# The last value group of a PEER layer: block by block over eight banks, with its norm's rows read earlier

## The chip, the cores and the metric

One core of one Trainium2 chip. The metric is the device time of one execution in microseconds (us); lower is better. TensorE multiplies matrices, VectorE and ScalarE work on rows and columns in SBUF (on-chip memory) and PSUM (the eight banks that TensorE writes), GpSimd gathers rows, and SyncE's queue issues most of the transfers.

## What is computed

A decoder layer for 512 tokens of width 2048: a mixer of attention and a state space model, a first layer norm, and a PEER feed-forward layer with a second layer norm. The change touches the end of the last part:

```
h   = x * (1 + sc2) + sh2
act = gelu(h @ u_tab[ids].T)          # 128 picked experts of 16384 for each token
ffn = (g * act) @ v_tab[ids]
x   = LN2(ALPHA * x + (1 + g2) * ffn)  # mean, variance, gain, shift over 2048 columns
```

## The kernel before, in words

Tokens stand in four blocks of 128 (TB = 4). For three of them (DB = 3, 384 tokens) the feed-forward runs densely over all 16384 experts, as 128 tiles of 128 experts, with gates that are zero for experts not picked. The fourth block is done by gathered rows, and its norm ends earlier.

The 128 tiles go in 32 groups of 4 (GT = 4), and `stream()` makes every engine walk the same list of groups. A group of kind "full" has 16 units: four u units, four v units, four u, four v. A unit is 512 KB (128x1024 f32) of the table, loaded by SyncE's queue (L725) into one of four slots `raw` when an earlier unit's split (`unit_split`) has freed it. It is split into two fp32r parts: `unit_high` on ScalarE copies the high part (L1125), `unit_low` on VectorE subtracts (L1780), into `split[:, j % 2]`. The high part of unit j waits until unit j-2 is used. A u unit is half the contraction of one tile of experts (matmuls L2212, bank 6 or 7, weights `h2_parts`). A v unit (L2276) is one tile of experts and one half of the 2048 output columns: 18 matmuls of 512 columns, three row blocks of six, added up in banks 0 to 5 (`bank_of`: block m in banks 2m and 2m+1). After four v units VectorE adds the banks to `out4` (`add_values`, L1710), counted by `v_read`, and TensorE's next unit waits for each block's read. In VectorE's `group()` the second half of a group is added at j = 0 to 3 of the next.

The last group ("last") has only the eight v units of the tiles before: units 0 to 3 are the left half of the columns, 4 to 7 the right half. TensorE runs unit by unit, each over the three blocks. `add_values` of the left half stands at j = 4. When SyncE has issued all loads and the full groups are used, it reads the first norm's output rows of the three blocks (`x1_back`, 3 MB, in the space of `h2_parts`, L733). VectorE's in-order list then is:

```
unit_low(5); first_half(0); unit_low(6); first_half(1); unit_low(7); first_half(2)
second_prepared(0..2)
second_half(0); second_half(1); finished(0); second_half(2); finished(1); finished(2)
```

`first_half(m)` (L1747, L1748, L1554) waits for `x1_back`, multiplies the left half of a row block by the gate row `g2b`, adds `x1_back`, and takes statistics of it. `second_prepared` (L1754, L1755) does the product and the sum for the right half. `second_half` (L1845, L1846) waits for all eight units, multiplies the right half's banks by the gate, adds, takes statistics and calls `spread` (L1422 to L1424). ScalarE takes the square root (`spread_root`, L1050). `finished` (L1561 to L1563, L1567, L1568) refines the root and applies mean, gain and shift; SyncE stores the rows. `own(...)` is an operation that VectorE waits for before the next.

## Time and profile before

| | us |
|---|---|
| median of 3 timed runs | 3253.71 (3250.67 to 3255.66) |
| the profiled execution | 3245.96 |
| its span in the trace | 3244.2 |
| granted TensorE clock, mean | 0.983 of 2.4 GHz |
| last u unit used, last unit of the full groups used, last matmul | 3147.5, 3164.95, 3204.94 |
| VectorE's last operation | 3239.92 |

The page gives busy times over the whole span. Since several stages with different limits follow each other, the end is read from three other views: the chain of waits in order of time (what released the work that ended last), the timeline (what ran when, and what ended an idle time), and busy times in stretches. All times of the trace are from the span's start.

### The profile page before, as it was taken

Reading aid. Unit: us, or ns where it says so; the run is one execution under the profiler, and the core shown is the slowest. Engines: PE = TensorE matmul, PEld = TensorE weight load, DVE = VectorE, ACT = ScalarE, POOL = GpSimd, SP = SyncE. Lnnn points to the kernel's source line nnn. Section 1 sums busy time; section 2 is a strip of 40 time slices with the busy share of each in tenths; the row PEclk is TensorE's granted clock in tenths of the full one; section 3 lists DMA queues with packets and bytes.
Section 4 is the critical chain, followed back from the end, with each engine's and each line's share of the span. In section 5 each row is a group of like instructions: output and inputs, shape, how many; then the busy total and the mean of one; then the engine's idle time right before and its main releaser. Section 6 shows DMA issues by size and latency. Waiting matters only on the chain.

```text
span 3244.2 us, 43813 instructions
## 1 busy us (share of the span) xinstructions
PE 3109.5 (96%) x16016; PEld 2659.8 (82%) x16016; DVE 2455.2 (76%) x3452; ACT 1056.3 (33%) x1632; POOL 1026.5 (32%) x734
## 2 busy tenths in 40 slices
PE   6999999999999999999999999999999999999994
PEld 4778887666469999997777899998999999999983
DVE  2397655645639999978888777888888888888757
ACT  1323545422223334332223333333333323333331
POOL 0110000000026553523222233435555554545200
PEclk9999999999999999999999999999999999999997
DMA  9786114465144555459888888888999899988853
GB/s 363 283 297 227 59 59 158 167 242 187 56 155 136 181 169 196 155 196 336 284 295 284 273 275 297 301 309 319 341 336 338 303 333 337 337 314 325 286 174 117
DMA packets 277725, 795.07 MB, mean 245 GB/s; under 512 B 118272, under 2 KB 138960, under 8 KB 230864
## 3 DMA queue, kind: packets, MB, share of 16 engines
q1 hardware_dynamic: 218816, 465.73, 42.6%
q0 software_dynamic: 50560, 317.87, 26.2%
q10 hardware_dynamic: 8208, 9.56, 0.8%
q8 instruction: 92, 1.51, 0.2%
q14 instruction: 49, 0.40, 0.0%
HBM read 750.07 MB, written 43.02 MB: 244 GB/s over the span
## 4 chain that ended last, share of the span: by engine, by line
PE 75%; DVE 18%; DMA 3%; issue 2%; ACT 1%; SPq 0%; POOL 0%; DVEq 0%; POOLq 0%; ACTq 0%
PE ps L2276 28%; PE ps L2212 26%; PE ps L1935 12%; DVE arena L1685 4%; PE ps L2187 3%; DVE arena L1682 2%; DMA arena<-in_w_ada 1%; DVE arena L1263 1%; PE ps L1959 1%; DVE arena L1710 1%; DVE split L1780 1%; PE ps L1894 1%; PE ps L1994 1%; PE ps L1871 1%; DVE win_parts L1250 1%
## 5 line engine op out<-in xcount | busy, mean ns | idle before, releaser
L2276 PE MATMUL ps<-split,w_parts 128*128 128x512 f32 x4608 | 1070.9, 392 | 20.0 <-DVE split L1780 17.2
L2276 PEld LDWEIGHTS ps<-split,w_parts 128*128 128x128 f32 x4608 | 863.8, 188 | 216.8 <-DVE split L1780 19.0
L2212 PE MATMUL ps<-h_parts,split 128*128 128x384 f32 x5376 | 947.4, 335 | 2.0 <-POOL split L788 1.4
L2212 PEld LDWEIGHTS ps<-h_parts,split 128*128 128x128 f32 x5376 | 933.7, 188 | 5.9 <-issue 1.6
L1125 ACT ACTIVATE split<-below_parts 128x1024 fp32r<-128x1024 f32 x416 | 441.7, 1062 | 1203.3 <-PE ps L2276 711.6
L1780 DVE TENSOR_TENSOR split<-below_parts,split 128x1024 fp32r<-128x1024 f32 x416 | 509.2, 1224 | 256.7 <-ACT split L1125 251.7
L800 POOL COPY arena<-arena 128x1 uint32 x256 | 209.8, 819 | 694.8 <-DVE arena L1734 389.4
L1715 DVE CUSTOM_DVE_ANT_0 arena<-arena 128x2048 f32<-128x2048 f32 x128 | 293.2, 2291 | 22.8 <-DMA arena<-in_u_tab,arena 22.8
L1734 DVE SCALAR_TENSOR_TENSOR arena<-arena 128x2048 f32<-128x2048 f32 x128 | 300.6, 2349 | 4.3 <-DVE arena L1726 2.2
L803 POOL DMA_INDIRECT arena<-in_v_tab,arena x128 | 257.4, 2011 | 104.4 <-POOL arena L800 103.1
L1250 DVE TENSOR_TENSOR win_parts<-arena,win_parts 128x512 fp32r<-128x512 f32 (+2 forms) x208 | 128.3, 629 | 210.5 <-ACT win_parts L854 201.3
L788 POOL TENSOR_TENSOR split<-below_parts,split 128x1024 fp32r<-128x1024 f32 x64 | 174.5, 2727 | 324.1 <-ACT split L1088 324.1
L803 POOL DMA_INDIRECT arena<-in_u_tab,arena x128 | 232.3, 1815 | 109.1 <-POOL arena L800 102.1
L1710 DVE TENSOR_TENSOR arena<-arena,ps 128x1024 f32<-128x1024 f32 x189 | 225.9, 1215 | 29.0 <-PE ps L2276 29.0
L1935 PE MATMUL ps<-win_parts,h_high_part 128*128 128x512 f32 (+1 forms) x640 | 198.7, 379 | 6.3 <-DVE win_parts L1250 4.2
L854 ACT ACTIVATE win_parts<-arena 128x512 fp32r<-128x512 f32 (+2 forms) x208 | 117.0, 576 | 194.1 <-PE ps L1935 187.5
L1685 DVE TENSOR_SCALAR arena<-iota,arena 128x128 f32<-128x128 f32 x384 | 169.5, 511 | 0.0
L755 POOL DMA_DIRECT2D arena<-in_w_slices x56 | 29.8, 533 | 406.0 <-DVE win_parts L1250 406.0
L1935 PEld LDWEIGHTS ps<-win_parts,h_high_part 128*128 128x128 f32 x640 | 118.4, 189 | 31.2 <-DVE win_parts L1250 7.5
L2212 PE MATMUL ps<-h_parts,w_parts 128*128 128x384 f32 x768 | 139.6, 336 | 0.9 <-PE ps L1959 0.6
L1935 PE MATMUL ps<-h_high_part,win_parts 128*128 128x512 f32 x384 | 132.9, 410 | 5.3 <-DVE h_low_part L1238 5.3
L2212 PEld LDWEIGHTS ps<-h_parts,w_parts 128*128 128x128 f32 x768 | 133.0, 188 | 1.7 <-issue 1.0
(275 smaller groups left out, 3221.2 us busy)
## 6 DMA issues: line engine op xcount, KB each, us to landing
below_parts<-in_u_units SPq DMA_DIRECT2D x256, 512.0 KB, 4.7
below_parts<-in_v_tab SPq DMA_DIRECT2D x256, 512.0 KB, 6.9
arena<-in_w_ada SPq DMA_DIRECT2D x96, 1024.0 KB, 7.2
arena<-in_w_slices POOLq DMA_DIRECT2D x56, 512.0 KB, 4.6
gates_by_expert<-arena SPq DMA_DIRECT2D x24, 1024.0 KB, 4.8
below_parts<-gates_by_expert SPq DMA_DIRECT2D x32, 768.0 KB, 9.1
arena<-in_w_out POOLq DMA_DIRECT2D x32, 512.0 KB, 5.5
acts_ahead<-arena ACTq DMA_DIRECT2D x48, 192.0 KB, 2.1
```

Source lines behind the costliest of these rows:

```text
L788: nc.gpsimd.tensor_tensor(part[:, 1, :], pre_raw[:, n % PRE_RAWS, :], part[:, 0, :].bitcast(F32), ALU.subtract).then_inc(pre_split, 1)
L800: nc.gpsimd.tensor_copy(idx[:, slot:slot + 1], ids[:, DB, bass.ds(pick, 1)]).then_inc(idx_copied, 1)
L803: nc.gpsimd.indirect_dma_start(out=ring[slot], out_offset=None, in_=table[:, :], in_offset=bass.IndirectOffsetOnAxis(ap=idx[:, slot:slot + ...
L1125: nc.scalar.activation(split[:, j % 2, 0, :], raw[:, j % RAWS, :], ACT.Copy).then_inc(high_done, 1)
L1685: ins = nc.vector.tensor_scalar(hot[:, 1, t, :], iota[:, :], pick_cols[:, 1, at_t:at_t + 1], pick_cols[:, 2, at_t:at_t + 1], ALU.is_equal, ...
L1710: nc.vector.tensor_tensor(row, row, wide(g.bank_of(-half if before else half, m), UNIT), ALU.add).then_inc(v_read, 1)
L1715: nc.vector.tensor_tensor_reduce(out=ring[slot], in0=ring[slot], in1=h2_now, scale=1.0, scalar=0.0, op0=ALU.mult, op1=ALU.add, accum_out=a ...
L1734: nc.vector.scalar_tensor_tensor(acc_v, ring[slot], w4[:, q:q + 1], acc_v, ALU.mult, ALU.add).then_inc(row_used, 1)
L1780: nc.vector.tensor_tensor(split[:, j % 2, 1, :], raw[:, j % RAWS, :], split[:, j % 2, 0, :].bitcast(F32), ALU.subtract)\
L1935: return nc.tensor.matmul(ps[:, bank_at, 0:cols], lhs, rhs, start=first and q == 0, stop=last and q == 2)
L2212: ins = nc.tensor.matmul(ps[:, 6 + b, 0:DT], lhs[:, cols], h2_parts[:, rhs, k, :], start=k == 0 and n == 0, stop=k == KT - 1 and n == 2)
L2276: ins = nc.tensor.matmul(ps[:, g.bank_of(half, m) + b, :], w_parts[:, buf, lhs, i, m * P:(m + 1) * P], rhs[:, b * 512:(b + 1) * 512], star ...
```

## The change

It concerns the last group and the norm behind it.

- SyncE issues the read of `x1_back` behind the load of the last group's unit 0, as soon as unit 11 (the last u unit) of the last full group is used.
- `prepared(m)` does product and sum of whole rows (2048 columns) before any unit of the last group is added, at j = 1, 2, 3, behind the split of that unit.
- The units 5 and 6 are split into spare space behind `x1_back`, so that their splits wait for no unit; unit 7 waits for units 0 to 3.
- TensorE does units 0 to 3 as before, in banks 6/7, 0/1, 2/3; then the right half block by block, all four units for block 0, 1 and 2, in banks 4/5, 6/7, 0/1.
- `half_whole(g, half, m)` multiplies a block's half out of PSUM by the gate and adds it to the row, with an operation that also gives the sum of the result. It takes the place of `add_values`, `second_half` and the statistics. `row_mean` makes the mean of the two sums.
- ScalarE gives the sum of squares about the mean (Square with the negative mean as bias and a sum over the row), written over `x1_back`; `row_spread` makes the variance of it.
- Two semaphores are replaced by counts of others (`gate_row_ps` by `gate_row`, `firsts_set` by `c_made`), with the same waits.

The diff, without the last of these:

```diff
@@ -287,6 +287,8 @@
+        if self.kind == "last" and half >= 0:
+            return (6 - 2 * half + 2 * m) % 8
         turned = self.c if half >= 0 else self.c - 1
@@ -531,6 +533,13 @@
         gated_part = at(PARTS + WP + UP + DB * D, UNIT)
+        spare_split = [h2_parts.rearrange("p a b c -> p (a b c)")[:, DB * D + UNIT + 2 * UNIT * i:DB * D + UNIT + 2 * UNIT * (i + 1)]
+                       .rearrange("p (a b) -> p a b", a=2) for i in range(2)]
+
+        def split_of(g, j):
+
+            return spare_split[j - 5] if g.kind == "last" and j in (5, 6) else split[:, j % 2, :, :]
+
         gate_tile = arena[0:3 * KT, LATER_ACC:LATER_ACC + P]
@@ -723,14 +732,15 @@
                     sp.dma_start(raw[:, slot, :], what.rearrange("a p n -> (a p) n")).then_inc(raw_full[slot], 16)
+                    if g.kind == "last" and j == 0:
+                        sp.wait_ge(unit_used, Group("full", GROUPS - 1, at_share=3).unit(12))
+                        sp.dma_start(x1_back, x1_out[:, 0:DB, :]).then_inc(x1_moved, 16)
                 if g.second:
...
-            sp.wait_ge(unit_used, Group("last", GROUPS).unit(0))
-            sp.dma_start(x1_back, x1_out[:, 0:DB, :]).then_inc(x1_moved, 16)
             for n, m in enumerate(TAIL):
@@ -1120,9 +1130,11 @@
                     act.wait_ge(pre_used, EARLY - 2 + j)
-                else:
+                elif g.kind == "last" and j == 7:
+                    act.wait_ge(unit_used, g.unit(4))
+                elif not (g.kind == "last" and j in (5, 6)):
                     act.wait_ge(unit_used, g.unit(j - 1))
-                nc.scalar.activation(split[:, j % 2, 0, :], raw[:, j % RAWS, :], ACT.Copy).then_inc(high_done, 1)
+                nc.scalar.activation(split_of(g, j)[:, 0, :], raw[:, j % RAWS, :], ACT.Copy).then_inc(high_done, 1)
@@ -1172,6 +1184,8 @@
             for n, m in enumerate(TAIL[1:]):
+                act.wait_ge(row_whole, n + 1)
+                nc.scalar.activation(x1_back[:, m, :], out4[:, m, :], ACT.Square, bias=mv[:, m, 1:2], accum_out=spread_of[:, m:m + 1]).then_inc(row_squared, 1)
                 spread_root(m, 2 * TB + 1 + n)
@@ -1738,21 +1752,36 @@
-            def first_half(m):
+            def prepared(m):
...
                     dve.wait_ge(x1_moved, 32)
-                    dve.wait_ge(v_read, (2 * GROUPS - 1) * DB)
-                part = out4[:, m, 0:UNIT]
-                own(nc.vector.tensor_tensor(part, part, g2b[:, 0:UNIT], ALU.mult))
-                own(nc.vector.tensor_tensor(part, part, x1_back[:, m, 0:UNIT], ALU.add))
-                half_stats(m, out4[:, m, :], 0)
-
-            def second_prepared(m):
-
-                part = out4[:, m, UNIT:]
-                own(nc.vector.tensor_tensor(part, part, g2b[:, UNIT:], ALU.mult))
-                own(nc.vector.tensor_tensor(part, part, x1_back[:, m, UNIT:], ALU.add))
+                    dve.wait_ge(v_read, (2 * GROUPS - 2) * DB)
+                row = out4[:, m, :]
+                own(nc.vector.tensor_tensor(row, row, g2b, ALU.mult))
+                own(nc.vector.tensor_tensor(row, row, x1_back[:, m, :], ALU.add))
+
+            def half_whole(g, half, m):
+
+                dve.wait_ge(unit_used, g.unit(4 + half * (m + 1)))
+                cols = slice(half * UNIT, (half + 1) * UNIT)
+                part = out4[:, m, cols]
+                nc.vector.tensor_tensor(gated_part, wide(g.bank_of(half, m), UNIT), g2b[:, cols], ALU.mult).then_inc(v_read, 1)
+                dve.wait_ge(v_read, g.val(2 * DB, (half - 1) * DB + m + 1 - DB))
+                own(nc.vector.tensor_tensor_reduce(out=part, in0=part, in1=gated_part, scale=1.0, scalar=0.0,
+                                                   op0=ALU.add, op1=ALU.add, accum_out=stats[:, m, half, 0:1]))
+
+            def row_mean(m):
+
+                left, right = stats[:, m, 0, 0:1], stats[:, m, 1, 0:1]
+                nc.vector.tensor_scalar(mv[:, m, 0:1], left, right, 1.0 / D, ALU.add, ALU.mult)
+                nc.vector.tensor_scalar(mv[:, m, 1:2], left, right, -1.0 / D, ALU.add, ALU.mult).then_inc(row_whole, 1)
+
+            def row_spread(m):
+
+                dve.wait_ge(row_squared, m + 1)
+                own(nc.vector.tensor_scalar(spread_of[:, m:m + 1], spread_of[:, m:m + 1], 1.0 / D, EPS, ALU.mult, ALU.add))
+                nc.vector.reciprocal(inv_root[:, m:m + 1], spread_of[:, m:m + 1]).then_inc(var_ready, 1)
@@ -1777,7 +1806,7 @@
                 dve.wait_ge(high_done, g.unit(j + 1))
-                nc.vector.tensor_tensor(split[:, j % 2, 1, :], raw[:, j % RAWS, :], split[:, j % 2, 0, :].bitcast(F32), ALU.subtract)\
+                nc.vector.tensor_tensor(split_of(g, j)[:, 1, :], raw[:, j % RAWS, :], split_of(g, j)[:, 0, :].bitcast(F32), ALU.subtract)\
                     .then_inc(unit_split, 1)
@@ -1812,7 +1841,7 @@
                                 add_values(g, 1, m, g.unit(0), True)
-                            if j == 4:
+                            if j == 4 and g.kind != "last":
                                 add_values(g, 0, m, g.unit(4))
@@ -1827,31 +1856,29 @@
                         gathered_block(j)
-                    if g.kind == "last" and j >= 5:
-                        first_half(j - 5)
+                    if g.kind == "last" and 1 <= j <= DB:
+                        prepared(j - 1)
+                    if g.kind == "last" and j == 7:
+                        for m in range(DB):
+                            half_whole(g, 0, m)
...
-            for m in range(DB):
-                second_prepared(m)
-
-            def second_half(m):
-
-                dve.wait_ge(unit_used, Group("last", GROUPS).unit(8))
-                part = out4[:, m, UNIT:]
-                own(nc.vector.tensor_tensor(gated_part, wide(2 * m, UNIT), g2b[:, UNIT:], ALU.mult))
-                own(nc.vector.tensor_tensor(part, part, gated_part, ALU.add))
-                own(half_stats(m, out4[:, m, :], 1))
-                spread(m)
-
-            second_half(0)
-            second_half(1)
+            last = Group("last", GROUPS)
+            half_whole(last, 1, 0)
+            row_mean(0)
+            half_whole(last, 1, 1)
+            row_mean(1)
+            row_spread(0)
             finished(0)
-            second_half(2)
+            row_spread(1)
+            half_whole(last, 1, 2)
+            row_mean(2)
             finished(1)
+            row_spread(2)
             finished(2)
@@ -2256,6 +2283,8 @@
                 for j, (table, i, half) in enumerate(g.units):
+                    if g.kind == "last" and half:
+                        continue
                     pe.wait_ge(unit_split, g.unit(j + 1))
@@ -2269,13 +2298,30 @@
                                 pe.wait_ge(pre_gelu, AHEAD * GT)
-                            if i == 0 and not (g.second and (half == 0 or m == 0)):
+                            if i == 0 and g.kind == "last":
+                                if m == 0:
+                                    pe.wait_ge(tile_gelu, g.val(GT, 2 - AHEAD * GT))
+                                else:
+                                    pe.wait_ge(v_read, g.val(2 * DB, m - 3 * DB))
+                            elif i == 0 and not (g.second and (half == 0 or m == 0)):
                                 pe.wait_ge(v_read, g.val(2 * DB, (half - 2) * DB + m - DB + (0 if g.kind == "ahead" else 1)))
...
                     ins.then_inc(unit_used, 1)
+                if g.kind == "last":
+                    for m in range(DB):
+                        pe.wait_ge(v_read, g.val(2 * DB, m - 2 * DB))
+                        for i in range(GT):
+                            j = GT + i
+                            pe.wait_ge(unit_split, g.unit(j + 1))
+                            high, low = split_of(g, j)[:, 0, :], split_of(g, j)[:, 1, :]
+                            for n, (lhs, rhs) in enumerate(((0, high), (0, low), (1, high))):
+                                for b in range(2):
+                                    ins = nc.tensor.matmul(ps[:, g.bank_of(1, m) + b, :], w_parts[:, buf, lhs, i, m * P:(m + 1) * P], rhs[:, b * 512:(b + 1) * 512],
+                                                           start=i == 0 and n == 0, stop=i == GT - 1 and n == 2)
+                        ins.then_inc(unit_used, 1)
```

## Rows read from the trace of the kernel before

**Rows 1.** The page: span, and busy time of each engine.
```profile
span 3244.2 us, 43813 instructions
...
PE 3109.5 (96%) x16016; PEld 2659.8 (82%) x16016; DVE 2455.2 (76%) x3452; ACT 1056.3 (33%) x1632; POOL 1026.5 (32%) x734
```

**Rows 2.** The chain of waits, 3050 to 3245 us: start us, us, what.
```profile
3177.62 12.23 DMA arena<-x_rows
3189.88 1.24 DVE arena L1747
```

**Rows 3.** The timeline of the last group: start us, us, engine, line, operation [idle before <-releaser].
```profile
3164.99 3.48 DVE L1710 TENSOR_TENSOR arena<-arena,ps 128x1024 f32<-128x1024 f32 x3 [1.70 <-PE ps L2276]
...
3166.36 16.61 PE L2276 MATMUL ps<-split,w_parts 128*128 128x512 f32 x72 [1.41 <-DVE arena L1710]
3168.39 1.22 DVE L1780 TENSOR_TENSOR split<-below_parts,split 128x1024 fp32r<-128x1024 f32 x1
...
3193.60 1.21 DVE L1780 TENSOR_TENSOR split<-below_parts,split 128x1024 fp32r<-128x1024 f32 x1
3193.99 1.28 ACT L1050 ACT_TABLE_LOAD   x1
3194.72 1.22 DVE L1747 TENSOR_TENSOR arena<-arena 128x1024 f32<-128x1024 f32 x1
...
3194.86 10.08 PE L2276 MATMUL ps<-split,w_parts 128*128 128x512 f32 x36 [2.04 <-DVE split L1780]
```

**Rows 4.** The timeline of the tail.
```profile
3210.82 1.23 DVE L1845 TENSOR_TENSOR arena<-ps,arena 128x1024 f32<-128x1024 f32 x1
3212.08 1.23 DVE L1846 TENSOR_TENSOR arena<-arena 128x1024 f32<-128x1024 f32 x1
...
3215.14 0.16 DVE L1424 RECIPROCAL arena<-arena 128x1 f32<-128x1 f32 x1
3215.22 1.21 DVE L1845 TENSOR_TENSOR arena<-ps,arena 128x1024 f32<-128x1024 f32 x1
...
3229.28 0.20 DVE L1561 SCALAR_TENSOR_TENSOR arena<-arena 128x1 f32<-128x1 f32 x1
...
3234.55 0.21 DVE L1561 SCALAR_TENSOR_TENSOR arena<-arena 128x1 f32<-128x1 f32 x1
...
3237.57 2.35 DVE L1568 SCALAR_TENSOR_TENSOR arena<-arena 128x2048 f32<-128x2048 f32 x1
```

**Rows 5.** Two rows of the timeline, and the value loads' row of the DMA view.
```profile
3147.48 4.28 PE L2276 MATMUL ps<-split,w_parts 128*128 128x512 f32 x18
...
3152.35 25.23 SPq L725 DMA_DIRECT2D below_parts<-in_v_tab  x7
...
below_parts<-in_v_tab SPq DMA_DIRECT2D x12, 512.0 KB, 4.1
```

**Rows 6.** Groups on VectorE by shape: operation xcount | busy us, mean ns.
```profile
L1715 DVE CUSTOM_DVE_ANT_0 arena<-arena 128x2048 f32<-128x2048 f32 x128 | 293.2, 2291 | 22.8 <-DMA arena<-in_u_tab,arena 22.8
...
L1715 DVE DVE_READ_ACCUMULATOR2_ANT arena<- 128x1 f32 x128 | 10.6, 83 | 0.0
...
L1762 DVE TENSOR_TENSOR arena<-arena 128x2048 f32<-128x2048 f32 x1 | 2.3, 2282 | 0.0
```

**Rows 7.** ScalarE: a group of 2048 columns, and the timeline of an Exp (L908) and a Square (L914).
```profile
L974 ACT ACTIVATE arena<-arena 128x2048 f32<-128x2048 f32 x1 | 1.9, 1917 | 0.0
...
535.65 0.63 ACT L908 ACTIVATE arena<-arena 128x512 f32<-128x512 f32 x1
536.18 0.62 ACT L914 ACTIVATE arena<-arena 128x512 f32<-128x512 f32 x1
536.71 0.18 ACT L914 ACTIVATION_READ_ACCUMULATOR arena<-arena 128x1 f32 x1
```

**Rows 8.** Busy time in stretches; PEclk, DMA share and GB/s last.
```profile
3148.00:3165.00 17.00, 16.34 (x71) 12.82 (x69) 9.29 (x10) 4.88 (x6) 0.00 (x0) 1.00 0.39 118
...
3196.00:3198.00 2.00, 2.00 (x6) 1.60 (x5) 1.97 (x3) 0.00 (x0) 0.00 (x0) 0.50 0.03 8
```

More of the change, by code:

```diff
@@ L567, in decoder_layer @@
             "cols_ps cols_ready hot_ready g_ps g_staged pre_high pre_split pre_used pre_gelu high_done unit_split unit_used "
-            "tile_gelu w_made w_high w_ready v_read picks_w tail_loaded gate_row_ps gate_row gate_stored ada_row firsts_set x1_ready y_ready "
+            "tile_gelu w_made w_high w_ready v_read picks_w tail_loaded row_whole gate_row gate_stored ada_row row_squared x1_ready y_ready "
             "out_done var_ready root_ready"
@@ L577, in decoder_layer @@
          pre_high, pre_split, pre_used, pre_gelu, high_done, unit_split, unit_used, tile_gelu, w_made, w_high, w_ready, v_read,
-         picks_w, tail_loaded, gate_row_ps, gate_row, gate_stored, ada_row, firsts_set, x1_ready, y_ready, out_done, var_ready,
+         picks_w, tail_loaded, row_whole, gate_row, gate_stored, ada_row, row_squared, x1_ready, y_ready, out_done, var_ready,
          root_ready) = map(sem, names.split())
@@ L646, in _ @@
                 weights(slot, w_q[slot, :, :])
-            sp.wait_ge(gate_row, 1)
+            sp.wait_ge(gate_row, 2)
             sp.dma_start(rows_out[:, :], gate_tile).then_inc(gate_stored, 16)
@@ L981, in beside @@
                 if n == TURNED + 1:
-                    act.wait_ge(gate_row_ps, 1)
+                    act.wait_ge(gate_row, 1)
                     nc.scalar.activation(gate_tile, ps[0:3 * KT, 6, 0:P], ACT.Copy).then_inc(gate_row, 1)
@@ L1189, in _ @@
             own(nc.vector.tensor_tensor(firsts[:, :], firsts[:, :], ident[:, 64:65], ALU.add))
-            nc.vector.tensor_tensor(firsts[:, :], firsts[:, :], ident[:, 96:97], ALU.add).then_inc(firsts_set, 1)
+            nc.vector.tensor_tensor(firsts[:, :], firsts[:, :], ident[:, 96:97], ALU.add).then_inc(c_made, 1)
             dve.wait_ge(small_loaded, 9 * 16)
@@ L2138, in beside @@
                     pe.wait_ge(mod_ready, CHUNKS + MODS - 2)
-                    turn(ps[0:3 * KT, 6, 0:P], mod_cols[:, 3 * KT:6 * KT]).then_inc(gate_row_ps, 1)
+                    turn(ps[0:3 * KT, 6, 0:P], mod_cols[:, 3 * KT:6 * KT]).then_inc(gate_row, 1)
             pe.wait_ge(c_made, 2)
@@ L2144, in _ @@
             pe.wait_ge(consts, 18)
-            pe.wait_ge(firsts_set, 1)
+            pe.wait_ge(c_made, 3)
             chunk_mod_sums(0)
@@ L2171, in _ @@
                 if m == 0:
-                    pe.wait_ge(gate_row, 1)
+                    pe.wait_ge(gate_row, 2)
                 if m == 1:
```

## The prediction, made before the changed kernel was run

> **What bounds the kernel now.** The page comes first: TensorE is busy 96% of the span, VectorE 76% [rows 1]. The change touches only the last value group and what follows it, about 80 of 3244 us, so the page's averages say little about it. The chain of waits of the last 200 us [rows 2] shows the bound change hands: it runs through TensorE until the splits of the last group, then through the transfer that reads the first norm's rows back (12.2 us, landed at 3189.85), and from 3189.88 through VectorE alone, to 3239.92. The timeline of the last group [rows 3] shows why. From 3164.99 VectorE has three additions and the seven splits of units 1 to 7, but the work of the norm must wait for that transfer, issued only at 3177.62, behind seven value loads. When it lands, 50 us of VectorE work are left and only 15 us of TensorE's (it ends at 3204.94). In the timeline of the tail [rows 4] the operations follow each other with no gap: product out of PSUM, sum, two statistics, the small steps, the two steps of the affine. So time is won by VectorE work that is removed or comes before 3189.88, and TensorE has slack.
>
> **What the change moves.** The transfer is issued once the last u unit is used, which is when TensorE begins the next value unit, at 3147.48 [rows 5], 30 us sooner. It stands in SyncE's queue behind the load of the last group's unit 0 and ahead of loads 1 to 7, of which the first goes at 3152.35 [rows 5]. With the old 12.2 us it lands at 3159.8. If load 1 ran wholly behind it, with the 4.1 us median of these loads [rows 5], it would land at 3163.9; ScalarE needs it when the full group's last unit is used, at 3164.95. So this costs nothing; the cover is 1.1 us by that worst sum, and without it each us late would be a us late for unit 1. The semaphores that are merged (c_made, gate_row) have the same waits and cost nothing.
>
> **VectorE's list after the change**, from the same start, 3164.99 [rows 3]:
> - The three additions, to 3168.39.
> - Seven splits at a pitch of 1.14 us (3193.60 to 3194.72 in [rows 3] is 1.12): 8.0.
> - Three times prepared(): two products or sums of 2048 columns, 2.28 us each [rows 6] plus 0.03 to the next, 4.62: 13.9. They stand after splits 1, 2 and 3, so all splits are out at 3168.39 + 8.0 + 13.9 = 3190.3.
> - Six times half_whole(): a product out of PSUM at a pitch of 1.26 [rows 4], and a sum that also adds up the row. No row has that operation at 1024 columns. The same operation at 2048 takes 2.29 plus an accumulator read of 0.08, and goes at the pitch of the plain 2048 one [rows 6]. Between 1.07 (2.29 - 1.22, what 1024 columns more cost) and 2.29 (the 2048 price) I take 1.25, the plain 1024 pitch. 2.51 each, 15.1.
> - Three row_mean() at 0.2 and three row_spread() at 0.27, from the 0.16 us of a one-column step, and 0.08 to the next where none waits [rows 4]: 1.4.
> - Three finished(), 5.3 each by the step from 3229.28 to 3234.55 [rows 4]: 15.9.
> - Waits on ScalarE. The Square of 2048 columns lies between 1.9 (an ACTIVATE of 2048) and 2.5 (four of 512, 0.63 each); with the 0.18 of the accumulator's read on the lower one I take 2.1 [rows 7]. For rows 1 and 2 it ends beside half_whole() or finished(). For row 0 it starts as row_mean(0) ends and has only half_whole(1,1), 2.7 us, for cover, which holds; then the table for Sqrt has to be loaded, 1.28 us, as it was behind the last Copy before [rows 3], and here behind the first Square. That load ends 0.5 us later than row_spread(0): with the root itself 0.7. For row 2 the root's round trip is open, 0.3. Row 1's is covered. Sum 1.0.
>
> In order: 3190.3 + 15.1 + 1.4 + 15.9 + 1.0 = 3223.7, against 3239.92 before. **The gain is 16.2 us.** Behind the last operation stand 4.3 us of output transfer up to the span's end, unchanged.
>
> What is left out as covered, with the cover. Before, four units of the first half took TensorE 16.61 us [rows 3], 4.15 each, or 5.54 for a block of 24 matmuls. After, unit 0 starts 1.4 us sooner, since its first block goes to banks that nothing reads. Units 1, 2 and 3 then wait for splits that come behind prepared(): starts at 3169.6, 3175.4 and 3181.2, end at 3185.4 instead of 3182.97. Nothing waits for that: the high part of unit 7 needs it, is done 1.1 us later, and VectorE reaches split 7 only at 3189.2. TensorE's blocks of the second half then end at 3192.6, 3198.1 and 3203.7, while VectorE wants them at 3197.9, 3200.6 and 3209.7: the covers are 5.3, 2.5 and 6.0 us. The value load of unit 7 is issued at split 3, 3181.2, and with 4.1 us is there by 3185.4, when ScalarE is free for it. The finished rows' output transfers are 5 to 8 us apart and cost only the last one.
>
> **The clock** is where the trace speaks against the change. TensorE idled 2.04 us ahead of unit 6, and its granted clock fell to 1.2 GHz (0.50 from 3196 to 3198, [rows 8]), with 6 matmuls in 2 us instead of 8 or 9, before it was back at 2.4. After the change it waits 1.6 us ahead of each of units 2, 3 and 4. I expect one or two such falls, each worth 1 to 2 us of TensorE's time; in the first half a unit at the lower clock takes up to 8.3 us instead of 5.8, and still ends before split 7 is reached. The covers above hold one fall. The Trainium skill (TensorE: Matmul & The Clock Gate, HAM oscillation — how this bites in real kernels) says that a matmul loop whose bursts are cut by waits can fall back to the low clock each time and start each burst cold; by that rule the half-clock case is the likely one, which is the first rival. By this trace the clock came back under continuous matmuls, and the second half is continuous.
>
> The Trainium skill (ScalarE: Activation LUTs, Table sets: the hidden batching unit) has cheap functions in every table set but does not list Square among the examples; if it weren't there, one more load of 1.28 us would stand ahead of the first Square, where ScalarE is idle. The trace has a Square straight behind an Exp with no load between [rows 7], so the sum has none.
>
> **Against which time.** The profiled execution took 3245.96 us, span 3244.2, and would take 3229.8. It lies below the three timed runs (3250.67 to 3255.66, median 3253.71), so the forecast for the median is 3253.71 - 16.2 = **3237.5**.
>
> **Rivals.**
> 1. TensorE at half clock through the second half. A matmul costs 0.231 us at full clock (16.61/72), so 0.46, a block 11.1: blocks end at 3198.1, 3209.2 and 3220.3. VectorE then does half_whole(1,1) at 3209.2 to 3211.9, finished(0) to 3218, half_whole(1,2) from 3220.3 to 3223.0, finished(1) to 3228.3 and finished(2) to 3234.2. Gain 5.8, median 3248. For it: the three waits. Against it: the recovery in [rows 8] with matmuls running. 0.05.
> 2. ScalarE becomes a link of every row: its Square, a table load each way and the root, 2.1 + 2.6 + 0.3 = 5.0, open three times instead of the 1.0 I count. Gain 16.2 - 14.0 = 2.2, median 3251.5. For it: Square and Sqrt alternate. Against it: work for another row stands between, and Square needed no table. 0.05.
> 3. Slower: VectorE's wait for the norm rows now stands ahead of split 2, with TensorE behind it. Before, a late transfer delayed only the norm. If it lands after 3169.5, every us is a us of the end. It decides against the change when it lands later than 3169.5 + 16.2 + 6.5 = 3192.2, 44.7 us after its issue; there the time is 3260. For it: 3 MB beside loads that TensorE needs. Against it: 12.2 us before, beside a value load and a 1 MB output, and a DMA share of 0.39 in the stretch where it will run [rows 8]. 0.02.
> 4. The change does not do what it says: the rows come sooner but the splits behind prepared() starve TensorE so that it, not VectorE, ends the list. By the covers above this needs 5 us more per unit. It would give back about half, 3246. 0.03.
>
> **How the numbers follow.** The forecast's case has 0.85. About 0.2% (6.5 us) is what a measurement of this kernel can tell from no change. Cases 1 and 2 are within it, case 4 is faster by a little more: faster 0.87, same 0.10, slower 0.03 (case 3 and what I overlook). The range: below, the small steps and waits at nothing (-2.4) and the sum at 1.07 (-1.1) with a run that is 1 to 2 us low give 3232; above, the summing operation at its upper bound (six times 1.04, +6.2) gives 3243.7, and the spread of the runs, 2 us, reaches into case 4: 3246.
>
> **What would show it.** The transfer of the rows landing before 3165; splits 2 and 3 at 5.8 us from each other with TensorE waiting for them; all splits out by 3190.3; VectorE without gaps from 3165 to about 3224; half_whole's sum at 1.25; one Sqrt table load behind the first Square; TensorE done near 3204. It is wrong if VectorE waits for TensorE in the second half, if the summing operation is near 2.3, or if VectorE waits for the rows.

## The result and the profile after

| | before | after |
|---|---|---|
| first timing, median | 3252.32 us (4 runs, 3250.67 to 3255.66) | 3231.64 us (4 runs, 3225.60 to 3235.09) |
| ratio of that timing | | 0.9931, 95% interval 0.9908 to 0.9955 |
| all timings of the study, mean | 3248.8 us (101 runs, 3237.0 to 3260.7, standard deviation 5.1) | 3231.4 us (15 runs, 3225.6 to 3236.7, standard deviation 3.3) |
| ratios of the two repeats | | 0.9934 (0.9913 to 0.9955), 0.9955 (0.9938 to 0.9973) |
| the profiled execution, and its span | 3245.96, 3244.2 | 3231.71, 3229.9 |
| from the last full group's additions to the span's end ("the tail") | 79.2 | 63.3 |

The kernel is faster by 0.45 to 0.7%, as forecast in direction. The forecast was 3237.5 in a range from 3232.0 to 3246.0; the median of 3231.64 lies 0.4 us below that range. The tail is used below as a measure of its own: from the start of the three additions of the last full group's right half (3164.99 before, 3166.58 after) to the end of the span. What lies ahead of it is called upstream.

The page of the changed kernel, for [rows 1]. TensorE's and VectorE's sums hardly move: VectorE has 6 us less work in 2455, which does not say where the 16 us went.

```profile
span 3229.9 us, 43815 instructions
...
PE 3107.5 (96%) x16016; PEld 2657.1 (82%) x16016; DVE 2449.4 (76%) x3446; ACT 1062.0 (33%) x1638; POOL 1028.7 (32%) x734
```

The timeline of the changed kernel's last group, for [rows 3] and [rows 5] (start us, us, engine, line, operation [idle before <-releaser]). L737 is the rows' transfer, L734 the value loads, L1809 the splits, L1761 and L1762 prepared().

```profile
3149.30 0.33 SPq L737 DMA_DIRECT2D arena<-x_rows  x1
...
3153.98 29.15 SPq L734 DMA_DIRECT2D below_parts<-in_v_tab  x7
...
3166.58 3.48 DVE L1724 TENSOR_TENSOR arena<-arena,ps 128x1024 f32<-128x1024 f32 x3 [1.70 <-PE ps L2310]
...
3171.11 2.29 DVE L1761 TENSOR_TENSOR arena<-arena 128x2048 f32<-128x2048 f32 x1
...
3175.76 1.22 DVE L1809 TENSOR_TENSOR split<-below_parts,split 128x1024 fp32r<-128x1024 f32 x1
...
3177.04 4.42 PE L2310 MATMUL ps<-split,w_parts 128*128 128x512 f32 x18 [1.41 <-DVE split L1809]
...
3181.55 1.22 DVE L1809 TENSOR_TENSOR split<-below_parts,split 128x1024 fp32r<-128x1024 f32 x1
...
3187.34 1.22 DVE L1809 TENSOR_TENSOR split<-below_parts,split 128x1024 fp32r<-128x1024 f32 x1
3187.76 1.06 ACT L1137 ACTIVATE split<-below_parts 128x1024 fp32r<-128x1024 f32 x1 [3.25 <-DMA below_parts<-in_v_tab]
...
3188.71 1.62 PE L2322 MATMUL ps<-split,w_parts 128*128 128x512 f32 x6 [1.47 <-DVE split L1809]
...
3190.75 1.22 DVE L1809 TENSOR_TENSOR split<-below_parts,split 128x1024 fp32r<-128x1024 f32 x1
3191.89 1.22 DVE L1769 TENSOR_TENSOR arena<-ps,arena 128x1024 f32<-128x1024 f32 x1
...
arena<-x_rows SPq DMA_DIRECT2D x1, 3072.0 KB, 10.4
```

The rows' transfer goes at 3149.30 and takes 10.4 us. At 3171.11, when prepared(0) wants the rows, they have been there for 11 us, and from 3166.58 to 3191.89 VectorE has no gap. The splits come 5.8 us apart (3175.76, 3181.55, 3187.34), with TensorE waiting 1.4 us for each of them; the last one is out at 3191.89, where the first half_whole starts, 25.3 us behind the additions. Before, VectorE was busy for 13.3 us in the same stretch (3164.99 to 3190.30) and idle for 12.0. TensorE's right half starts at 3188.71, and the last block ends at 3205.3.

The timeline of the changed kernel's tail, for [rows 4] and [rows 6]: L1769 is the product, L1771 the sum with its accumulator read, L1188 the Square, L1060 the root and its table.

```profile
3193.14 1.23 DVE L1771 CUSTOM_DVE_ANT_0 arena<-arena 128x1024 f32<-128x1024 f32 x1
3194.29 0.08 DVE L1771 DVE_READ_ACCUMULATOR2_ANT arena<- 128x1 f32 x1
3194.41 1.23 DVE L1769 TENSOR_TENSOR arena<-ps,arena 128x1024 f32<-128x1024 f32 x1
...
3202.36 2.01 ACT L1188 ACTIVATE arena<-arena 128x2048 f32<-128x2048 f32 x1 [13.54 <-DVE arena L1778]
...
3204.47 1.28 ACT L1060 ACT_TABLE_LOAD   x1
...
3206.00 0.22 DVE L1575 SCALAR_TENSOR_TENSOR arena<-arena 128x1 f32<-128x1 f32 x1 [0.65 <-ACT arena L1060]
...
3220.20 0.22 DVE L1575 SCALAR_TENSOR_TENSOR arena<-arena 128x1 f32<-128x1 f32 x1 [0.27 <-ACT arena L1060]
...
3223.23 2.35 DVE L1582 SCALAR_TENSOR_TENSOR arena<-arena 128x2048 f32<-128x2048 f32 x1
```

The sum over 1024 columns takes 1.23 us, a pair of product and sum 2.52 (3191.89 to 3194.41). The only waits of VectorE in the tail are 0.65 us ahead of 3206.00, where the table load for the root stands behind the first Square, and 0.27 ahead of 3220.20.

The slices of the granted clock, for [rows 8] (PEclk is the third number from the end):

```profile
3164.00:3182.00 18.00, 15.67 (x66) 11.67 (x64) 16.16 (x11) 3.62 (x4) 0.00 (x0) 1.00 0.29 93
3182.00:3188.00 6.00, 4.42 (x18) 3.30 (x18) 5.93 (x4) 2.75 (x4) 0.00 (x0) 1.00 0.68 198
3188.00:3206.00 18.00, 16.60 (x72) 13.44 (x72) 16.97 (x26) 4.43 (x6) 0.00 (x0) 1.00 0.06 22
```

The clock stayed at 2.4 GHz up to the last matmul.

### The profile page after: what moved, and what is told of

It reads as the page before. It is cut to its first block, busy times and chain, and to the rows that moved or that the text cites. A ratio compares the mean times of both kernels' runs of the same rounds, so it can differ in the third digit from the quotient of the medians.

```text
span 3229.9 us, 43815 instructions
## 1 busy us (share of the span) xinstructions
PE 3107.5 (96%) x16016; PEld 2657.1 (82%) x16016; DVE 2449.4 (76%) x3446; ACT 1062.0 (33%) x1638; POOL 1028.7 (32%) x734
## 4 chain that ended last, share of the span: by engine, by line
PE 73%; DVE 18%; DMA 4%; issue 3%; ACT 1%; POOL 1%; SPq 0%; DVEq 0%; POOLq 0%; ACTq 0%
PE ps L2310 26%; PE ps L2239 25%; PE ps L1962 12%; DVE arena L1699 4%; PE ps L2214 3%; DVE arena L1696 2%; DMA arena<-in_w_ada 1%; DVE arena L1724 1%; DVE arena L1277 1%; PE ps L1986 1%; DVE split L1809 1%; DMA arena<-in_u_tab,arena 1%; PE ps L1921 1%; PE ps L2021 1%; PE ps L1898 1%
## 5 line engine op out<-in xcount | busy, mean ns | idle before, releaser
L2310 PE MATMUL ps<-split,w_parts 128*128 128x512 f32 x4536 | 1054.7, 392 | 19.1 <-DVE split L1809 19.1
L2310 PEld LDWEIGHTS ps<-split,w_parts 128*128 128x128 f32 x4536 | 849.9, 188 | 213.5 <-DVE split L1809 20.9
L1809 DVE TENSOR_TENSOR split<-below_parts,split 128x1024 fp32r<-128x1024 f32 x414 | 506.6, 1224 | 254.4 <-ACT split L1137 249.7
L813 POOL DMA_INDIRECT arena<-in_v_tab,arena x128 | 264.1, 2063 | 104.4 <-POOL arena L810 103.1
L813 POOL DMA_INDIRECT arena<-in_u_tab,arena x128 | 223.2, 1744 | 109.1 <-POOL arena L810 101.3
```

Of the source, the lines that this page charges most:

```text
L813: nc.gpsimd.indirect_dma_start(out=ring[slot], out_offset=None, in_=table[:, :], in_offset=bass.IndirectOffsetOnAxis(ap=idx[:, slot:slot + ...
L1809: nc.vector.tensor_tensor(split_of(g, j)[:, 1, :], raw[:, j % RAWS, :], split_of(g, j)[:, 0, :].bitcast(F32), ALU.subtract)\
L2310: ins = nc.tensor.matmul(ps[:, g.bank_of(half, m) + b, :], w_parts[:, buf, lhs, i, m * P:(m + 1) * P], rhs[:, b * 512:(b + 1) * 512], star ...
```

## The experiments

Each was timed in turn with the kernel before on the same chip. "Tail" is from its profiled execution.

| kernel | tail, us | median, us (runs) | before beside it | ratio, 95% interval |
|---|---|---|---|---|
| before, again | 79.8 | 3246.64 (12) | 3248.14 | 0.9995, 0.998 to 1.001 |
| changed, again | 63.3 | 3230.79 (6) | 3248.14 | 0.9934, 0.9913 to 0.9955 |
| semaphores alone | 79.5 | 3249.33 (12) | 3248.14 | 1.0008, 0.9991 to 1.0024 |
| early transfer alone | 76.9 | 3245.73 (12) | 3248.14 | 0.9989, 0.9976 to 1.0002 |
| early rows, old order | 76.7 | 3249.62 (10) | 3249.60 | 0.9995, 0.9981 to 1.0009 |
| changed, old statistics | 70.2 | 3241.32 (10) | 3249.60 | 0.9973, 0.996 to 0.9987 |
| changed, rows late | 78.5 | 3250.32 (10) | 3249.60 | 1.0005, 0.9993 to 1.0018 |
| changed, one block on GpSimd | 70.1 | 3238.90 (7) | 3249.60 | 0.9969, 0.995 to 0.9989 |
| before, new sums | 73.0 | 3243.07 (11) | 3249.30 | 0.998, 0.9967 to 0.9993 |
| changed, a third time | 63.4 | 3232.75 (5) | 3249.30 | 0.9955, 0.9938 to 0.9973 |
| changed, left half sooner | 59.5 | 3230.21 (7) | 3249.30 | 0.9959, 0.9942 to 0.9975 |
| the same again | 59.5 | 3227.68 (6) | 3245.64 | 0.9936, 0.992 to 0.9953 |

### Was there a gain ahead of the last group?

The first timing gave a gain of 20.7 us, the tails 15.9. Theory A: the tail is the gain and the rest is scatter. Theory B: some 5 us came from upstream, for which only the replaced semaphores are there. Three kernels were run: both once more, and the kernel before with this part of the change alone:

```diff
-            pe.wait_ge(firsts_set, 1)
+            pe.wait_ge(c_made, 3)
...
-                    turn(ps[0:3 * KT, 6, 0:P], mod_cols[:, 3 * KT:6 * KT]).then_inc(gate_row_ps, 1)
+                    turn(ps[0:3 * KT, 6, 0:P], mod_cols[:, 3 * KT:6 * KT]).then_inc(gate_row, 1)
```

together with the other places that name these semaphores.

> The kernel before, once more, as its own control. The stretch from the last group's additions to the end of the span was 79.2 us in the first trace (3164.99 to 3244.2); what lies ahead of it is the upstream part. Theory A (the last group alone changed, the rest is scatter of the upstream part): ratio 1.000 within 0.001, tail 79.2 within 0.5 us, upstream anywhere from 3160 to 3175. Theory B (the timed runs of before are really some 5 us longer than a profiled one): the profile is again shorter than the timed median by 5 us or more.

> The changed kernel, once more. Its tail was 63.3 us in the first trace (3166.58 to 3229.9), 15.9 less than before. Theory A (the change is worth what its tail shows): ratio 0.9951 (-15.9 us), between 0.9940 and 0.9962, tail 63.3 within 0.5. Theory B (the change also shortens something ahead of the last group by 5 us, as the first timing's 0.9931 would say): ratio 0.993 or less with a tail of 63.3 and an upstream part that is 5 us or more below that of the control.

> The kernel before with the change's two replaced semaphores alone (gate_row_ps by counts of gate_row, firsts_set by counts of c_made). Theory A: they cost and bring nothing, ratio 1.000 within 0.001, tail 79.2. Theory B (the missing 5 us come from here, the only part of the change that lies ahead of the last group): ratio 0.9985, upstream part 5 us shorter.

The span and the start of the additions, first in the second profile of the kernel before, then in that of the changed kernel:

```profile
span 3241.9 us, 43813 instructions
...
3162.12 3.48 DVE L1710 TENSOR_TENSOR arena<-arena,ps 128x1024 f32<-128x1024 f32 x3 [1.70 <-PE ps L2276]
```

```profile
span 3232.8 us, 43815 instructions
...
3169.52 3.48 DVE L1724 TENSOR_TENSOR arena<-arena,ps 128x1024 f32<-128x1024 f32 x3 [1.70 <-PE ps L2310]
```

Tails of 79.8 and 63.3 again; the semaphores alone give 79.5 and no change of the time. The upstream parts were 3162.1 before and 3169.5 after: in these two profiles the changed kernel reached its last group 7 us later, and is faster all the same. So theory B has nothing for it in the profiles. Nor was its prediction of a profile shorter than its timed median by 5 us met (3243.7 against 3246.6).

What theory A had wrong is the size of the scatter. It expected the changed kernel's ratio between 0.9940 and 0.9962 and the control's within 0.001 of 1; the changed kernel's second ratio, 0.9934, lies outside, nearer to theory B's 0.993, and the control's interval is 0.003 wide with 12 runs against 29. The 101 runs of the kernel before spread over 24 us. The median of the three runs that the forecast started from, 3253.71, was 5 us above their mean, and the 3252.32 of the first timing was 3.5 above it.

A third timing of the changed kernel:

> The changed kernel a third time, for a tighter ratio and as the neighbour of left_sooner. Theory A: tail 63.3, ratio 0.9951 by the tails, and an interval that holds it; theory B (a real gain of 20 us or more): interval wholly below 0.9945.

Its tail was 63.35, its interval holds 0.9951. By all runs the means differ by 17.4 us, with a standard error of 1.0; by the profiles' tails the mean difference is 16.2 (79.2, 79.8 and 79.5, the last with the semaphores alone, against 63.3 three times). The two differ by 1.2 us, about one standard error, and whether one of the 17 us comes from elsewhere stays open.

Why the upstream part scatters stays open. One thing that varies in it is what ScalarE waits for. The waits of ScalarE on value loads between 1200 and 1900 us, in the profile with the shortest upstream part and in the one with the longest (waited for: us in total, times, longest):

```profile
ACT split L1125 <- DMA below_parts<-in_v_tab: 14.3, 4, 4.2
```

```profile
ACT split L1125 <- DMA below_parts<-in_v_tab: 107.5, 27, 8.2
```

14.3 against 107.5 us of waits go with additions that start at 3162.1 (before, again) and at 3178.8 (before, new sums). These parts of the two programs are the same. But the waits do not put the profiles between these two in order: the kernel with one block on GpSimd has 111.1 us of them and starts its additions at 3167.06, the changed kernel's second profile has 23.9 us and starts them at 3169.52. The mean granted clock of an execution goes with its time too: of the runs of the kernel before beside the experiments, the 10 at 0.982 took 3254.2 us on average and the 14 at 0.986 took 3244. Which of the two is a cause, and how much each one brings, was not tested.

### The early transfer alone

```diff
+                    if g.kind == "last" and j == 0:
+                        sp.wait_ge(unit_used, Group("full", GROUPS - 1, at_share=3).unit(12))
+                        sp.dma_start(x1_back, x1_out[:, 0:DB, :]).then_inc(x1_moved, 16)
...
-            sp.wait_ge(unit_used, Group("last", GROUPS).unit(0))
-            sp.dma_start(x1_back, x1_out[:, 0:DB, :]).then_inc(x1_moved, 16)
```

> The kernel before with only the transfer of the first norm's rows issued behind the load of the last group's unit 0; VectorE's list stays as it was. Theory A (VectorE's list sets the end, and earlier rows help only as far as work is placed to use them): first_half(0) starts behind the split of unit 5 instead of at the landing, 2.3 us sooner, tail 76.9 us, ratio 0.9993. Rival (the 3 MB ahead of the value loads starve TensorE in the last group): units 1 and 2 of the last group wait for their loads, tail above 79.2.

The timeline of this kernel's last group:

```profile
3170.09 3.48 DVE L1711 TENSOR_TENSOR arena<-arena,ps 128x1024 f32<-128x1024 f32 x3 [1.70 <-PE ps L2277]
...
3171.45 16.60 PE L2277 MATMUL ps<-split,w_parts 128*128 128x512 f32 x72 [1.41 <-DVE arena L1711]
...
3191.49 1.22 DVE L1781 TENSOR_TENSOR split<-below_parts,split 128x1024 fp32r<-128x1024 f32 x1
3192.63 1.22 DVE L1748 TENSOR_TENSOR arena<-arena 128x1024 f32<-128x1024 f32 x1
```

first_half(0) (at 3192.63) stands straight behind the split of unit 5; TensorE's four units of the left half go without a wait for a load, 16.60 us as before. The tail is 76.9 as theory A had it. Whether the late transfer also spread the timed runs can't be told: this kernel's runs have a standard deviation of 2.6 us, but those of the next one, which reads early too, have 4.8.

### Early rows in the old order

To the transfer above are added prepared() at j = 1, 2, 3 and, for the left half, product and sum at j = 4; TensorE's units, the banks and the statistics are those of before.

```diff
+            def first_added(g, m):
+                dve.wait_ge(unit_used, g.unit(4))
+                part = out4[:, m, 0:UNIT]
+                nc.vector.tensor_tensor(gated_part, wide(2 * m, UNIT), g2b[:, 0:UNIT], ALU.mult).then_inc(v_read, 1)
+                dve.wait_ge(v_read, g.val(2 * DB, m + 1 - 2 * DB))
+                own(nc.vector.tensor_tensor(part, part, gated_part, ALU.add))
```

> Rows read early and the product and sum of whole rows at j = 1, 2, 3, but TensorE's right half unit by unit over three banks pairs and the statistics as before. Theory A (earlier VectorE work pays only if TensorE's last half does not wait for it, which is what the block by block order over eight banks buys): VectorE must add the left half before unit 5 can go, TensorE ends 43 us behind the last group's additions, and VectorE waits some 5 us for it; tail 76.6 us, ratio 0.999. Rival (the early rows are the whole gain, the order and the banks bring nothing): tail about 68, ratio 0.9965.

```profile
3171.10 3.48 DVE L1711 TENSOR_TENSOR arena<-arena,ps 128x1024 f32<-128x1024 f32 x3 [1.70 <-PE ps L2279]
...
3191.85 1.22 DVE L1782 TENSOR_TENSOR split<-below_parts,split 128x1024 fp32r<-128x1024 f32 x1
...
3194.36 4.59 PE L2279 MATMUL ps<-split,w_parts 128*128 128x512 f32 x12 [2.64 <-DVE arena L1755]
...
3200.55 1.23 DVE L1782 TENSOR_TENSOR split<-below_parts,split 128x1024 fp32r<-128x1024 f32 x1
...
3207.39 1.23 DVE L1782 TENSOR_TENSOR split<-below_parts,split 128x1024 fp32r<-128x1024 f32 x1 [2.10 <-ACT split L1126]
...
3214.40 1.23 DVE L1848 TENSOR_TENSOR arena<-ps,arena 128x1024 f32<-128x1024 f32 x1 [4.59 <-PE ps L2279]
```

VectorE adds the left half from 3193.0 to 3200.5, between the splits of units 4 and 5; TensorE's fifth unit waits block by block for its reads (2.64 us ahead of 3194.36), and the split of unit 7 waits 2.1 us for ScalarE's copy, which waits for TensorE. TensorE is done only 43.3 us behind the additions, and the first second_half (at 3214.40) waits 4.6 us for it, as theory A had it. The tail is 76.7, no better than with the early transfer alone: 14 us of VectorE work moved ahead bought 0.2. So the earlier work counts only with a right half that doesn't wait for the left half's reads. Which part of that does it, the block by block order over further banks or the splits of units 5 and 6 that wait for no unit, was not told apart.

### The changed kernel without one part

Old statistics in the new order, without sums and Square:

```diff
-                own(nc.vector.tensor_tensor_reduce(out=part, in0=part, in1=gated_part, scale=1.0, scalar=0.0,
-                                                   op0=ALU.add, op1=ALU.add, accum_out=stats[:, m, half, 0:1]))
+                own(nc.vector.tensor_tensor(part, part, gated_part, ALU.add))
+                own(half_stats(m, out4[:, m, :], half))
```

> The changed kernel with the statistics of the kernel before: plain sum, two statistics per half and their aggregate, no row sums and no Square on ScalarE. Theory A (the list of VectorE sets the end, so each us of it counts): 7.7 us of statistics and 1.7 of aggregates come in, 2.4 of means, spreads and waits on ScalarE go; tail 70.2 us, ratio 0.9972. Rival (the tail hangs on ScalarE's Square and root): tail 63 or less.

```profile
3194.72 1.22 DVE L1767 TENSOR_TENSOR arena<-ps,arena 128x1024 f32<-128x1024 f32 x1
...
3197.23 1.29 DVE L1566 BATCH_NORM_STATS2 arena<-arena 128x6 f32<-128x512 f32 x2
3198.55 1.22 DVE L1767 TENSOR_TENSOR arena<-ps,arena 128x1024 f32<-128x1024 f32 x1
```

A block's half takes 3.83 us (3194.72 to 3198.55) instead of 2.52. The tail is 70.2, as expected.

The rows late, at the place of the kernel before:

```diff
-                    if g.kind == "last" and 1 <= j <= DB:
-                        prepared(j - 1)
+                    if g.kind == "last" and j >= 5:
+                        prepared(j - 5)
```

> The changed kernel with the transfer of the rows issued behind all value loads as before, and prepared() at j = 5, 6, 7. Theory A: the rows land 24 us behind the last group's additions, the first half_whole starts at 40 instead of 25.3, tail 78.2 us, ratio 0.9997. Rival (the new order and sums carry the gain, the rows' time matters little): tail below 70. If the rows' late landing is also what spreads the timed runs of the kernel before, its runs scatter by 5 us as those do, where the changed kernel's scatter by 3.

```profile
3166.37 3.48 DVE L1723 TENSOR_TENSOR arena<-arena,ps 128x1024 f32<-128x1024 f32 x3 [1.70 <-PE ps L2309]
...
3190.66 2.29 DVE L1760 TENSOR_TENSOR arena<-arena 128x2048 f32<-128x2048 f32 x1 [7.61 <-DMA arena<-x_rows]
...
3206.89 1.23 DVE L1768 TENSOR_TENSOR arena<-ps,arena 128x1024 f32<-128x1024 f32 x1
```

VectorE waits 7.6 us for the rows, the first half_whole starts 40.5 us behind the additions, and the tail is 78.5: of the 16 us, 1 is left. The runs have a standard deviation of 4.2 us, between the others, which decides nothing.

The new sums in the kernel before, with its order and its late rows:

```diff
-                own(nc.vector.tensor_tensor(part, part, gated_part, ALU.add))
-                own(half_stats(m, out4[:, m, :], 1))
-                spread(m)
+                own(nc.vector.tensor_tensor_reduce(out=part, in0=part, in1=gated_part, scale=1.0, scalar=0.0,
+                                                   op0=ALU.add, op1=ALU.add, accum_out=stats[:, m, 1, 0:1]))
```

and the same in first_half, with row_mean, Square and row_spread as in the change.

> The kernel before with the sums and the Square of the change in place of its statistics; order of units, banks and the rows' transfer as before. Theory A (VectorE's list is all that counts once the rows have landed): 7.7 us of statistics go, 0.9 us of waits on ScalarE come; tail 72.2 us instead of 79.2 to 79.8, ratio 0.9978. Rival (the operations that sum are worth something only in the new order): tail 77 or more.

The tail is 73.0 instead of 72.2: 6.5 us less than the 79.5 of before. In the new order the same exchange is worth 6.9 (70.2 to 63.3). The sums pay in either order. The early rows pay 15 us within the new order (78.5 to 63.3) and about 2.5 in the old one. Those 15 are not a gain over the kernel before: with late rows and the same sums the new order is 5.5 us worse than the old one (78.5 against 73.0), though that variant also does prepared() later than the change does. Early rows and new order together bring 9.7 us with the new sums (73.0 to 63.3) and 9.3 with the old statistics (79.5 to 70.2).

### Could the list be shorter still?

One block's product and sum on GpSimd, idle since the last gathered row:

```diff
+            row = out4[:, DB - 1, :]
+            pool.wait_ge(v_read, (2 * GROUPS - 2) * DB)
+            nc.gpsimd.tensor_tensor(row, row, g2b, ALU.mult).then_inc(idx_copied, 1)
+            pool.wait_ge(idx_copied, 2 * PICKS + 1)
+            nc.gpsimd.tensor_tensor(row, row, x1_back[:, DB - 1, :], ALU.add).then_inc(idx_copied, 1)
```

> The changed kernel with the product and sum of the third row block on GpSimd, which is idle there. Theory A (VectorE's list): it is 4.6 us shorter, of which 2.1 are lost since split 7 now waits for TensorE's unit 3 and ScalarE's copy; first half_whole 22.8 us behind the additions, tail 60.8, ratio 0.9943. Rival (the two engines slow each other at their memory port): VectorE's operations beside it take longer than 2.29 us, tail 63.3 or more.

```profile
3170.72 5.42 POOL L837 TENSOR_TENSOR arena<-arena 128x2048 f32<-128x2048 f32 x1 [116.61 <-DVE arena L1732]
...
3171.59 6.70 DVE L1769 TENSOR_TENSOR arena<-arena 128x2048 f32<-128x2048 f32 x1
...
3176.22 6.42 POOL L839 TENSOR_TENSOR arena<-arena 128x2048 f32<-128x2048 f32 x1
3178.32 6.47 DVE L1770 TENSOR_TENSOR arena<-arena 128x2048 f32<-128x2048 f32 x1
...
3185.96 2.28 DVE L1769 TENSOR_TENSOR arena<-arena 128x2048 f32<-128x2048 f32 x1
...
3186.10 10.17 PE L2320 MATMUL ps<-split,w_parts 128*128 128x512 f32 x36 [10.00 <-DVE split L1819]
```

The rival holds: the two engines slow each other, and the tail is 70.1 us, 6.8 longer than without the help. VectorE's product and sum took 6.70 and 6.47 us beside GpSimd's, and 2.28 once it was done; TensorE idled 10.0 us for the next split. The lengths fit a turn by turn use: GpSimd's first ends at 3176.14, VectorE's beside it 2.15 us later, at 3178.29; GpSimd's second ends at 3182.64, VectorE's at 3184.79, 2.15 later again. The Trainium skill (SBUF — State Buffer, Who interferes with whom) says that VectorE and GpSimd share a pair of ports under an exclusive lock, and that a VectorE instruction with two inputs in SBUF contends with a GpSimd instruction that reads SBUF. This trace agrees: both engines' operations here are plain f32 ones with two inputs in SBUF.

VectorE's idle time ahead of the additions, used for the left half of two blocks, which the last full group no longer changes:

```diff
+                        if j == 15:
+                            prepared(0, 0)
...
+                        if g.kind == "last" and j == 0:
+                            prepared(1, 0)
...
+                    if g.kind == "last" and 1 <= j <= 4:
+                        prepared(*((2, 0), (0, 1), (1, 1), (2, 1))[j - 1])
```

> The changed kernel with the left half's product and sum of two row blocks pulled ahead of the last group's additions, into VectorE's idle time, 2.5 us each, the rest in four pieces behind the splits 1 to 4. Theory A: 3.9 us leave the list behind the additions, the additions start up to 0.8 us later behind TensorE; tail 59.4 us, gain over the changed kernel 3.1 us, ratio to before 0.9942. Rival (the transfer lands too late, 10 to 13 us after its issue, and VectorE waits for it with TensorE's next splits behind it): the additions start 2 us or more later behind TensorE's last full unit, no gain.

> The version with the left half's work of two blocks pulled ahead, again, for its time. Its tail was 59.5 us, 3.9 less than the changed kernel's 63.3. Theory: ratio to before 0.9942 (tail 20.0 us below the 79.5 of before, less up to 0.8 us by which the additions start later), interval holding it. If what is pulled ahead only moves a wait to the part before the additions: ratio 0.9950 or more, as the changed kernel's.

```profile
3159.84 1.22 DVE L1764 TENSOR_TENSOR arena<-arena 128x1024 f32<-128x1024 f32 x1
...
3165.30 1.06 ACT L1137 ACTIVATE split<-below_parts 128x1024 fp32r<-128x1024 f32 x1 [3.02 <-PE ps L2317]
3166.04 3.48 DVE L1724 TENSOR_TENSOR arena<-arena,ps 128x1024 f32<-128x1024 f32 x3
...
3187.50 1.22 DVE L1772 TENSOR_TENSOR arena<-ps,arena 128x1024 f32<-128x1024 f32 x1
```

The first half_whole starts 21.5 us behind the additions (3187.50), and the tail is 59.5 in both profiles, as worked out. The additions start 0.74 us after ScalarE's copy that the same unit released (3165.30), where in the other kernels they start 0.06 ahead of it; so 3.1 of the 3.9 us are left, as expected. The two timings, 0.9959 and 0.9936, have intervals that overlap that of the changed kernel; the means of all runs are 3230.0 (13 runs) and 3231.4 (15), with a standard error of 1.7 for the difference. The trace shows the 3 us; the timed runs can't yet tell them from none.

## Why the prediction missed, step by step

**The mechanism and its sum held.** Worked out was a gain of 16.2 us; the tails give 15.9 for the first pair and 16.2 over all. Term by term, from the additions: all splits out after 25.3 us (predicted 25.3); a half_whole 2.52 (2.51), with the sum, for which there was no row, at 1.23 plus a read that overlaps, close to the value taken for it; finished() 5.28 to 5.38 (5.3); waits on ScalarE 0.65 and 0.27, together 0.9 (1.0); the table load once, behind the first Square; output 4.3. VectorE's last operation came 59.0 us behind the additions, 58.7 predicted.

**What was costed at nothing** cost nothing, with one cover used. The transfer landed at 3159.7, and unit 1's copy waited for TensorE, not for its load. The value load of unit 7 was late for ScalarE: its copy at 3187.76 waited for the load, 0.8 us longer than worked out (3185.4 and the 1.6 us by which this profile's additions start later), and VectorE came to that split only at 3190.75, as the cover said.

**The rivals.** Half clock (1): no fall occurred in the last group, though one or two were expected; the waits were 1.4 us and the clock held, in this profile and in the two further ones. The example in the section of the Trainium skill that the prediction cites there (TensorE: Matmul & The Clock Gate, HAM oscillation — how this bites in real kernels) has waits that are longer than these, so it did not make this case the likely one. ScalarE in every row (2): 0.9 us of waits in all. The rows late (3): the condition was not met, since they landed at 3159.7, 6.9 us ahead of the additions. The late variant lost 15 us, but it has prepared() behind other splits, so the rival's own case, late rows with prepared() at j = 1, was not run. TensorE starved (4): it waited 1.4 us three times and finished 6 us before its last block was read.

**The step that failed is "Against which time".** It put the forecast at the median of three runs less the gain, 3253.71 - 16.2, and gave the range 2 us for the spread of the runs. The runs of the kernel before have a standard deviation of 5.1 us (101 runs); from that, a median of three is off by some 3.4 us as a rule (an estimate, 5.1 times 0.67). The spread is all of it upstream as far as the profiles show (additions start between 3162.1 and 3178.8, the tails of one kernel agree within 0.6). With the base that 101 runs give, 3248.8, the same sum predicts 3232.6; 15 runs of the changed kernel have a mean of 3231.4. The warning stood in the text: a profiled execution 8 us below the three timed runs. It was named and set aside, and it was a draw from the same spread, as the three were. The same spread makes 0.2% too fine a bound for three or four runs.

## What to carry to other kernels

When one engine's in-order list sets the end, add up that list from a fixed event, and measure from that event to the end in the profile: here such a tail repeated within 0.6 us while whole runs spread by 24. Work moved ahead pays only if the engines that feed the rest are freed from it too, by banks and buffers that don't wait: early rows brought about 2.5 us in the old order, and together with the new order over 9; the new order with late rows lost 5.5. Give a forecast of the total the spread of the total, and compare a profiled execution with the timed ones before trusting the median of three.

## What the runs showed of the hardware beyond that

- Waits of TensorE of 0.4, 1.4 and 1.4 us, each followed by 4.4 us of matmuls, and one of 1.5 ahead of the right half left the clock at 2.4 GHz, in all three profiles of the changed kernel. In the kernel before, a wait of 2.04 us, 8.5 us after one of 1.4, was followed by a fall to 1.2 GHz ([rows 8]). But in its second profile the wait at the same place was longer, 2.63 us, and no fall followed; with the semaphores alone it was 2.29 us, and one did. So the length of the wait alone does not tell whether the clock falls. The second profile of the kernel before:

```profile
3192.57 4.37 PE L2276 MATMUL ps<-split,w_parts 128*128 128x512 f32 x18 [2.63 <-DVE split L1780]
...
3194.00:3198.00 4.00, 3.53 (x16) 2.58 (x16) 3.96 (x5) 0.00 (x0) 0.00 (x0) 1.00 0.00 0
```

- GpSimd and VectorE operations on f32 rows in SBUF took turns: VectorE's operations of 2.28 us took 6.70 and 6.47 beside GpSimd's.
- A sum over 1024 columns that goes with the addition costs hardly more of VectorE's time than the addition: pairs of product and sum of 2.52 us against 2.51 with the plain one (3194.72 to 3197.23 in the kernel with the old statistics).
- Square ran in the table set that was active, behind Copy and behind Sqrt, with no load of its own; only the first Sqrt loaded one, 1.28 us.
